# Preparing the first weights and norm tiles of the next projection beside each merge

## The reference, cut to what matters

```
def rms_norm(x, w):
    xf = x.astype(jnp.float32)
    xf = xf * lax.rsqrt(jnp.mean(xf * xf, axis=-1, keepdims=True) + EPS)
    return xf.astype(x.dtype) * w
...
    for layer in range(DEPTH):
        lambda_init = 0.8 - 0.6 * math.exp(-0.3 * layer)
        h = rms_norm(x, norm_pre[layer])
        proj = h @ w_in[layer]
...
        y = jnp.concatenate([y_a, y_b, y_c], axis=-1) @ w_out[layer]
        x = x + rms_norm(y, norm_post[layer])
    return x
```

```
    h = _rmsnorm(x, w['norm_w']) * (1.0 + scale[:, None]) + shift[:, None]
    hc = _rmsnorm(ctx, w['norm_w']) * (1.0 + scale_c) + shift_c
    na_q, na_k, na_v, na_z, dn_qkv, dn_z, dn_b, dn_a, g_na, g_dn = _split_proj(h @ w['w_in'])
```

## Time and profile before

| | |
|---|---|
| median of 3 runs | 3884.26 us (3882.74 to 3886.54) |
| profiled execution | 3915.89 us |
| its span | 3914.1 us, 82663 instructions |
| granted clock over the span | 0.885 |
| TensorE (PE) busy | 3250.0 us (83%) |
| VectorE (DVE) busy | 2134.9 us (55%) |
| ScalarE (ACT) busy | 1318.4 us (34%) |
| GpSimd (POOL) busy | 582.3 us (15%) |
| weight loads of the two projections | 1376.0 KB, 6.8 us to landing; 1792.0 KB, 10.8 us |

### The profile page before, as it was taken

One profiled execution on the slowest core, in us unless ns is written; L12 is line 12 of the kernel. 1 busy time (PEld: TensorE's weight loads), 2 busy tenths in 40 slices (PEclk: granted clock), 3 DMA queues, 4 the chain that ended last, 5 costly groups with the idle time before them and its releaser, 6 DMA issues. The chain is left out here.

```text
span 3914.1 us, 82663 instructions
## 1 busy us (share of the span) xinstructions
PE 3250.0 (83%) x36108; PEld 2689.5 (69%) x36108; DVE 2134.9 (55%) x3567; ACT 1318.4 (34%) x2374; POOL 582.3 (15%) x466
## 2 busy tenths in 40 slices
PE   7999977757799999545497998789999788887699
PEld 7988864543498888444345987778888577776244
DVE  3455538877425555579584255456665444544452
ACT  3133325534312333446243122234443121221441
POOL 0200004431001000245110012011110121221100
PEclk9999987778899999656698999889999688998799
DMA  4522222224335221231333444552331311111430
GB/s 134 170 90 71 82 64 70 75 101 136 119 102 182 69 76 48 57 79 37 125 123 127 145 161 136 171 165 92 110 111 38 102 43 39 47 39 35 173 105 32
DMA packets 270500, 379.79 MB, mean 97 GB/s; under 512 B 46389, under 2 KB 209517, under 8 KB 268792
## 3 DMA queue, kind: packets, MB, share of 16 engines
q1 hardware_dynamic: 168074, 261.54, 21.6%
q10 hardware_dynamic: 102066, 112.97, 8.4%
HBM read 257.46 MB, written 118.94 MB: 96 GB/s over the span
## 5 line engine op out<-in xcount | busy, mean ns | idle before, releaser
L366 PE MATMUL psum<-proj_w_low,h_high 128*128 128x344 f32 (+1 forms) x1984 | 668.5, 337 | 17.0 <-DVE proj_y L389 16.7
L366 PE MATMUL psum<-proj_w_high,h_low 128*128 128x344 f32 (+1 forms) x1984 | 658.2, 332 | 0.0
L366 PE MATMUL psum<-proj_w_high,h_high 128*128 128x344 f32 (+1 forms) x1984 | 657.6, 331 | 0.0
L366 PEld LDWEIGHTS psum<-proj_w_low,h_high 128*128 128x128 f32 x1984 | 376.7, 190 | 30.3 <-DVE proj_y L389 18.2
L366 PEld LDWEIGHTS psum<-proj_w_high,h_high 128*128 128x128 f32 x1984 | 376.6, 190 | 6.9
L366 PEld LDWEIGHTS psum<-proj_w_high,h_low 128*128 128x128 f32 x1984 | 375.9, 189 | 7.1
L366 PE MATMUL psum<-proj_rest_w_low,h_high 128*128 128x304 f32 x640 | 209.1, 327 | 33.8 <-DVE proj_rest_w_low L378 22.0
L1358 PE MATMUL psum<-w_out,merge_yt 128*128 128x512 f32 x512 | 228.3, 606 | 1.8 <-DVE merge_yt L1241 1.8
L802 POOL TENSOR_TENSOR scan_d<-scan_b 128x384 f32<-128x384 f32 x112 | 125.4, 1119 | 615.2 <-DVE scan_b L643 606.7
L389 DVE COPY proj_y<-psum 128x344 f32<-128x344 f32 (+1 forms) x130 | 70.5, 542 | 252.9 <-PE psum L366 252.7
L1102 DVE COPY diff_wt<-psum 128x512 f32<-128x512 f32 x64 | 44.3, 692 | 287.4 <-PE psum L1048 287.4
(11 more groups left out here) (408 smaller groups left out, 6872.8 us busy)
## 6 DMA issues: line engine op xcount, KB each, us to landing
proj_raw<-in_w_in SPq DMA_DIRECT2D x24, 1376.0 KB, 6.8
proj<-proj_y ACTq DMA_DIRECT2D x192, 172.0 KB, 1.9
delta_x<-dn_qkv SPq DMA_DIRECT2D x40, 384.0 KB, 5.2
proj<-proj_y ACTq DMA_DIRECT2D x68, 224.0 KB, 1.9
dn_prep_x<-proj SPq DMA_DIRECT2D x54, 256.0 KB, 3.3
proj_raw<-in_w_in SPq DMA_DIRECT2D x7, 1792.0 KB, 10.8
modulate_w<-in_mod_w SPq DMA_DIRECT2D x16, 768.0 KB, 4.7
merge_z<-proj SPq DMA_DIRECT2D x8, 1536.0 KB, 7.2
```

What stands on the lines that cost most here:

```text
L366: last = PE.matmul(self.ps[:, j % self.banks, 0:self.width], hp[:, kt, tokens], wp[:, c % 2, kt, :], start=kt == 0 and n == 0, stop=kt == ...
```

## The change

A new class `Ahead` runs as a second part beside each `Merge1`. Beside the merge of tiles 3 to 7 it issues, for the next stage: the first two weight loads, the norm's constants, the loads of norm tiles 0 and 1 (once the merge has stored them), the split of the first weights, and the scaling of norm tiles 0 and 1. `Norm` and `Project` get a count `begun` (2 tiles, 1 weight group), and leave out in their own stage what is begun. The second weight group is loaded ahead, too, and split in the next stage, due 2.4 and 3.2 items after the projection's start. In layer 1's stage the projection's start is 2.2 in place of 2.5, in the second block's 0.4 in place of 1; layer 0's stage has no `Ahead` and keeps 2.5. The buffers of `Project` are laid out as raw and w_low (the same address), w_high, y, in place of y, w_high, raw. Helper functions (`consts_in`, `load`, `act_scale`, `dve_scale`, `split_low`, `split_high`) hold code that stood in the generators.

```diff
-    def sp(self):
+        self.begun = 0
+
+    def consts_in(self):
         SP = self.nc.sync
         SP.dma_start(self.w[:], bc(self.weight, [P, D])).then_inc(*self.consts.inc())
         if self.shift is not None:
             SP.dma_start(self.b[:], bc(self.shift, [P, D])).then_inc(*self.consts.inc())
-        for t in range(self.n):
+
+    def load(self, t):
+        self.nc.sync.dma_start(self.x[:, t % 2], self.src[t * P:(t + 1) * P, :]).then_inc(*self.loaded[t % 2].inc())
+
+    def sp(self):
+        if not self.begun:
+            self.consts_in()
+        for t in range(self.begun, self.n):
             yield t - 1.5
             if t >= 2:
-                SP.wait_ge(*self.normed(t - 2))
-            SP.dma_start(self.x[:, t % 2], self.src[t * P:(t + 1) * P, :]).then_inc(*self.loaded[t % 2].inc())
+                self.nc.sync.wait_ge(*self.normed(t - 2))
+            self.load(t)
...
+    def act_scale(self, t):
+        S, s = self.nc.scalar, t % 2
+        S.wait_ge(*self.loaded[s](t // 2))
+        if t >= 2:
+            S.wait_ge(*self.transposed(t - 2))
+        S.activation(self.xn[:, s], self.x[:, s], ACT.Square, accum_out=self.ss[:, s:s + 1]).then_inc(*self.squared.inc())
+        S.wait_ge(*self.meant(t))
+        self.k.so.chain(S.activation(self.rs[:, s:s + 1], self.ss[:, s:s + 1], ACT.Ln))
+        S.activation(self.rs[:, s:s + 1], self.rs[:, s:s + 1], ACT.Exp, scale=-0.5).then_inc(*self.rstd.inc())
...
+                self.act_scale(t)
             if t:
                 split(t - 1)
         yield self.n
         split(self.n - 1)
+
+    def dve_scale(self, t):
+        V, s = self.nc.vector, t % 2
+        ss, rs, xn = self.ss[:, s:s + 1], self.rs[:, s:s + 1], self.xn[:, s]
+        V.wait_ge(*self.squared(t))
+        V.tensor_scalar(ss, ss, 1.0 / D, EPS, ALU.mult, ALU.add).then_inc(*self.meant.inc())
+        V.wait_ge(*self.rstd(t))
+        scaled = V.scalar_tensor_tensor(out=xn, in0=self.x[:, s], scalar=rs, in1=self.w[:], op0=ALU.mult, op1=ALU.mult)
+        if self.shift is None:
+            scaled.then_inc(*self.normed.inc())
+        else:
+            self.k.vo.chain(scaled)
+            V.tensor_tensor(xn, xn, self.b[:], ALU.add).then_inc(*self.normed.inc())
 
...
-        self.y = self.tile("y", [P, 4, width])
-        self.wh = self.tile("w_high", [P, 2, KT, width], F32R)
         self.raw = k.at(f"{name}_raw", [P, 2, KT, width], self.top)
         self.wl = self.tile("w_low", [P, 2, KT, width], F32R)
+        self.wh = self.tile("w_high", [P, 2, KT, width], F32R)
+        self.y = self.tile("y", [P, 4, width])
...
+        self.begun = 0
 
     def start(self, c):
 
-        return self.first[c - 1] if c >= 2 else 2 * c - 4
+        return self.first[c - 1] if c >= 2 else 0 if self.begun else 2 * c - 4
+
+    def load(self, c):
+        first = self.columns[c]
+        src = self.w[:, first:first + self.width].rearrange("(k p) n -> p k n", p=P)
+        self.nc.sync.dma_start(self.raw[:, c % 2], src).then_inc(*self.loaded[c % 2].inc())
 
     def sp(self):
-        SP = self.nc.sync
-        for c in range(len(self.groups)):
+        for c in range(2 if self.begun else 0, len(self.groups)):
             yield self.start(c) + 0.1
             if c >= 2:
-                SP.wait_ge(*self.product(self.first[c - 1] - 1))
-            first = self.columns[c]
-            src = self.w[:, first:first + self.width].rearrange("(k p) n -> p k n", p=P)
-            SP.dma_start(self.raw[:, c % 2], src).then_inc(*self.loaded[c % 2].inc())
+                self.nc.sync.wait_ge(*self.product(self.first[c - 1] - 1))
+            self.load(c)
...
     def dve_split(self):
+        for c in range(self.begun, len(self.groups)):
+            yield self.start(c) + 3.2
+            self.split_low(c)
+
+    def split_low(self, c):
         V = self.nc.vector
-        for c in range(len(self.groups)):
-            yield self.start(c) + 3.2
...
     def act_split(self):
+        for c in range(self.begun, len(self.groups)):
+            yield self.start(c) + 2.4
+            self.split_high(c)
+
+    def split_high(self, c):
         S = self.nc.scalar
-        for c in range(len(self.groups)):
-            yield self.start(c) + 2.4
-            S.wait_ge(*self.loaded[c % 2](c // 2))
...
+class Ahead(Stage):
+
+
+    def __init__(self, k, name, norm, project, merge):
+        super().__init__(k, name)
+        self.norm, self.project, self.merge = norm, project, merge
+        norm.begun, project.begun = 2, 1
+
+    def sp(self):
+        yield 3.2
+        self.project.load(0)
+        self.norm.consts_in()
+        for t in range(2):
+            yield 4.2 + t
+            self.nc.sync.wait_ge(*self.merge.stored[t](0))
+            self.norm.load(t)
+        yield 5.6
+        self.project.load(1)
+
+    def act(self):
+        yield 4.4
+        self.project.split_high(0)
+        for t in range(2):
+            yield 6.3 + t
+            self.norm.act_scale(t)
+
+    def dve(self):
+        yield 4.9
+        self.project.split_low(0)
+        yield 6
+        self.nc.vector.wait_ge(*self.norm.consts(self.norm.consts.total - 1))
+        for t in range(2):
+            yield 6.3 + t
+            self.norm.dve_scale(t)
+
+    def pe(self):
+        yield 0
+
+    pool = pe
...
+        def first_part(layer):
             h, above = h_t(f"h{layer}", T)
...
+            return norm, project, prepare, x
+        w2 = args["w_in_2"].rearrange("a k n -> (a k) n")
+        late = range(NCTX, NT2)
+        parts = first_part(0)
+        for layer in range(DEPTH):
+            norm, project, prepare, x = parts
             attention = DiffAttention(k, layer, p1, qk_t, o_diff, norm, project, prepare, prepare.top, 2)
-            together(k, (norm, 0, 1.0), (project, 2.5, 1.0), (prepare, 30.5, 1.5), (attention, 48, 1.6))
+            together(k, (norm, 0, 1.0), (project, 2.2 if layer else 2.5, 1.0), (prepare, 30.5, 1.5), (attention, 48, 1.6))
             low = k.bottom
...
             together(k, (states, 0, 1.0), *([(context, 0, 1.0)] if layer else []), (fetch, 0.5, 0.5))
             merge = Merge1(k, layer, p1, o_scan, o_diff, x, xs, wo, (hw, pw, dsc))
             assert merge.top <= room
-            together(k, (merge, 0, 1.0))
-        h, above = h_t("h2", T)
-        norm = Norm(k, "norm2", above, xs, NT, h, 0, mod[0:1, D:2 * D], mod[0:1, 0:D], 4)
-        w2 = args["w_in_2"].rearrange("a k n -> (a k) n")
-        late = range(NCTX, NT2)
-        project = Project(k, "proj2", above + 45056, h, [range(NT2)] * 6 + [late], w2, 448, p2, row_of=row2, normed=norm, ctx=h_ctx, order=(2, 3, 4, 5, 0, 1, 6))
+            if layer == 0:
+                parts = first_part(1)
+                ahead = Ahead(k, "ahead1", parts[0], parts[1], merge)
+                assert parts[0].top <= room and merge.top <= parts[1].bottom
+            else:
+                h, above = h_t("h2", T)
+                norm = Norm(k, "norm2", above, xs, NT, h, 0, mod[0:1, D:2 * D], mod[0:1, 0:D], 4)
+                project = Project(k, "proj2", above + 45056, h, [range(NT2)] * 6 + [late], w2, 448, p2, row_of=row2, normed=norm, ctx=h_ctx, order=(2, 3, 4, 5, 0, 1, 6))
+                ahead = Ahead(k, "ahead2", norm, project, merge)
+                assert project.bottom + 4 * KT * 448 * 3 <= room and merge.top <= norm.bottom
+            together(k, (merge, 0, 1.0), (ahead, 0, 1.0))
         early = DeltaPrepareLate(k, "dn_prep", [(tile, part) for part in range(3) for tile in range(6)], p2, dn, above, norm=norm, project=project)
         assert max(early.top, norm.top) <= above + 45056, early.top - above
         assert project.top <= end - 8 * KT * CTX, project.top
-        together(k, (norm, 0, 1.0), (project, 1, 1.0), (early, 22, 0.6))
```

33 lines of the change are left out of this document (9 added, 24 removed).

## The result

| | before | changed |
|---|---|---|
| median | 3885.40 us (3882.74 to 3888.76, 4 runs) | 3847.95 us (3839.85 to 3852.36, 4 runs) |
| ratio | | 0.9902, 95% interval 0.9880 to 0.9924 |
| profiled span | 3914.1 us | 3847.0 us |
| TensorE busy | 3250.0 us (83%) | 3210.8 us (83%) |
| VectorE busy | 2134.9 us (55%) | 2134.5 us (55%) |

The change saves 37 us (29 to 47 by the interval); the forecast was 34 and 3850. The two profiles differ by 67 us, 30 more than the runs, so the first thing is to see where the two spans differ. The marks are one and the same SP issue in every kernel: the first of the stage, and for the last two rows the first load of the rest's weights and of delta_x, which stand 1 to 3 us behind their stage's first issue.

The account below looks back on a forecast made before the run. Load chains behind both merges leave TensorE idle; behind them it is nearly always busy. Boundaries 16.1 + 20.9, less 2 for attention and 0.5 + 0.5 for copies, save 34.0 us: 3884.26 becomes 3850, range 3841 to 3866.

Parts of the forecast that it names:

- Holes: TensorE's load-chain gaps behind both merges: first projection matmul 17.8 us earlier in layer 1, 22.9 us in the second block.
- Lead: Projections of layer 1 and second block: preparation one item less ahead, so TensorE waits; -0.8 and -1.1 us.
- Cover: Inside both merges: preparation fits the slack before the last transposes, cost 0, with 0.9 and 0.5 us left.
- Attention of layer 1: Behind the first boundary: last RoPE transposes one item later against the first attention scores; -2 us, ends 0 and -4.
- Second block's copies: Projection copies ahead of the delta preparation: -0.5 us; earlier copies could take off up to 2.9, a colder phase add 6.
- The clock: At both boundaries: transposes count as work; rise at 1040 to 1042 at the first, +0 to +1 us; second 0.
- Sum: Whole kernel: 16.1 + 20.9 - 2 - 0.5 - 0.5 = 34.0 us saved, median 3884.26 becomes 3850.
- One sign of being wrong: Whole profile: the forecast would be wrong if the time moved elsewhere than in the two merges and two projection stages.
- B: Merges slip by 2 us each, or waits cost in full at projections, attention and copies; 3859 to 3868 us; chance 0.20.
- C: At both boundaries transposes don't wake the clock, or a gap restarts its count; gain 31 us, 3853; chance 0.12.
- D: At the boundaries second weights or third norm tile come late, or the barrier still waits for a load; 3880 to 3884; 0.04.
- E: Layer 1's projection and attention share PSUM banks, so TensorE waits in each of 32 attention steps; slower, 3900; chance 0.04.

Follow-up runs that it names:

- second split: Changed kernel with the second weight group of layer 1's projection also split beside the merge: 3842.01 us, 0.9856 of the kernel before.
- doubled pass: Changed kernel with one more VectorE pass over the first raw weights ahead of the low split in each merge: 3860.66 us, 0.9895 of the kernel before.
- first boundary alone: Kernel before with only the merge of layer 0 to projection of layer 1 prepared ahead, second block's start 1: 3862.70 us, 0.9953.
- old starts: Changed kernel with the projections' starts as before (2.5 and 1): 3845.05 us, 0.9910 of the kernel before.
- second boundary alone: Kernel before with only the merge of layer 1 to second block's projection prepared ahead, layer 1's start 2.5: 3859.25 us, 0.9945.
- layout alone: Kernel before with the projection's buffers in the new order, nothing prepared ahead, starts as before: 3881.35 us, 1.0003.

## Why the prediction was right, point by point

- **Holes.** 17.8 and 22.9 us earlier were forecast for the first projection matmul; 17.9 (22.43 to 4.52) and 23.0 (23.03 to 0.04) came. Right.
- **Lead.** -0.8 and -1.1 were forecast; the waits for scaled tiles were 1.0 (0.29 + 0.71, with 0.55 for a copy behind them) and 2.1. At the first boundary the cause is shown by the second split moved away; at the second that wasn't tried, and the term was 1.0 too small.
- **Cover.** 0 was forecast and 0 came; the margins, forecast as 0.9 and 0.5 us, were 1.2 and 0.8 by the doubled pass.
- **Attention of layer 1: -2 was wrong.** The last RoPE step does come an item later, but the first scores waited 4.22 us for their transfer, against 4.27. What stood there instead, in both profiles of the changed kernel: the 1.7 us that RoPE's transposes waited for VectorE are gone, and TensorE waits 2.4 us (2.3 in the second profile) at 1192.37 for a copy of the projection. By VectorE's order that copy now stands behind a RoPE step that waits for POOL; no run moved it away, so this cause is read from the trace and not tested. Seen so, the wait changed its name and grew by 0.7.
- **Second block's copies: -0.5 was wrong in sign.** They gave 4.0 us back (17.7 to 13.7). The forecast named a gain here ("up to 2.9") but set it against the risk of a colder phase, priced at 6, which did not come. The new start gives it, alone (12.6 us of copy waits left) and with everything else.
- **The clock: +0 to +1.** The forecast took transposes as work like other, and let the clock rise at 1040 to 1042, 6 to 8 us after the stage's first issue. It rose 3.2 us after the first of the 16 transposes, and 3.3 to 3.6 us after it in three other kernels with that begin (first boundary alone, second split, doubled pass), each time before the first projection matmul; in the second profile of the changed kernel it rose only 8.9 us after, and with the old starts it stood at 0.50 through all three groups. So transposes can bring the clock back and the identity's transposes hold it, but how soon it comes back the forecast couldn't know. The Trainium skill, page "TensorE: Matmul & The Clock Gate", section "Part 4: PE-mode transpose", says that in transpose mode a transpose doesn't count as a busy TensorE in the same way; the rows of these transposes, with the clock at 1.00 through 6.7 us of them, don't agree, and they decide here (which mode these transposes run in, no row tells).
- **Sum.** In stages, 14.0 + 27.6 = 41.6 in the first pair of profiles and 12.3 + 25.3 = 37.6 against the second profile of the changed kernel; in whole times 37 and 33; forecast 34.0. Put right, the sum reads: 34.0, plus 2.5 that attention and its copies' phases didn't cost, plus 4.5 for the second block's copies, less 1.2 (2.9 us of copy waits in layer 1 against RoPE's 1.7), less 1.2 more for the leads: 38.6. Two terms were too pessimistic, by 2.5 and 4.5 us, and costs of 2.4 us were missing; that these cancel in part is luck. The two holes, from which nearly all of the sum comes, came as worked out. In the first profile of the changed kernel the clock gave about 3 on top (half-speed stretches behind the first projection matmul 3.6 us shorter at one boundary and 2.7 at the other), in the second next to none. One sign of being wrong that the forecast had named did show in the profiles: 28 of the 67 us lie outside the four stages. These stages have the same instructions in both kernels, and the last section shows that they differ as much between profiles without any change.

Of the rivals, B, the preparation paid for in the merges, falls with merges of 152.6 and 152.3 us. C, the clock low for longer, holds in part for the second profile at the first boundary: 4.4 us at half speed behind the first projection matmul, where its price assumed 5.8. D and E, no effect and a longer wait in every attention step, did not come: TensorE's waits within attention's steps are 1.8 us in two places before and after.

## What to carry to other kernels

Where a stage begins with its own loads behind a barrier, look for the engine idle in the stage before: loads, splits and norms of the first tiles fit under a matmul-bound tail, and the gain is the hole, nearly whole, as long as the added step fits the slack between the last dependent step and the matmul that waits for it. Look at both what is begun and what is then the second of its kind: the second weights' split was the next thing that stuck. And when two orders meet (projection and preparation), shift one by less than an item and look at the copy waits: here 0.6 of an item took 4 to 5 us off them.

## What the runs showed of the hardware that was not expected

**Whole times move with the clock of a stage that nobody touched.** The delta rule's stage has the same instructions in all kernels. Before, in the changed kernel, and in the one with the second boundary alone:

```profile
3037.60:3614.80 577.20, 489.24 (x15564) 425.44 (x15564) 262.33 (x540) 112.18 (x242) 116.55 (x100) 0.85 0.19 48
```

```profile
2993.50:3547.50 554.00, 466.52 (x15564) 406.04 (x15564) 260.64 (x540) 112.18 (x242) 116.64 (x100) 0.89 0.20 50
```

```profile
3016.70:3551.60 534.90, 451.50 (x15564) 392.70 (x15564) 260.07 (x540) 112.07 (x242) 116.54 (x100) 0.93 0.20 51
```

Clock 0.85, 0.89, 0.93 and 577, 554, 535 us. That is 42 us between profiles, more than the change is worth, and it accounts for 23 of the 30 us by which the first two profiles differ more than the runs. The plainest case is the kernel before against the one with the layout alone, which are equally fast in their runs: spans of 3914.1 and 3869.8 us, 44 apart, of which 42 lie in this stage (576.9 and 534.9). What sets that clock is open; its matmuls are short ones with gaps.

**The clock's return differs with the same code.** The changed kernel was profiled twice. TensorE at the first boundary in the second profile (the first is shown with the result):

```profile
1039.56 3.65 PE L311 MATMUL psum<-ident,norm_xn 128*128 128x128 f32 x16 [7.41 <-PEq L179]
1044.03 0.63 PE L385 MATMUL psum<-proj_w_low,h_high 128*128 128x344 f32 x1 [0.83 <-DVE h_low L292]
```

In the first profile the clock was back 3.2 us after TensorE's first transpose, and the first projection matmul took 0.40 us. In the second it stood at 0.50 through the transposes and until 1048.5, the first projection matmul took 0.63 us, and layer 1's stage was 1.7 us longer. At the second boundary it was back 3.1 us after the first matmul in one and 5.2 in the other. A gain of one or two microseconds at such a place can't be read from one profile.
